# Dilation groups of a head pair in the order 1, 2, 0, and softmax denominators spread over the partitions through DRAM

## The reference, cut to what matters

```python
hn = rmsnorm(x, norm_g)
q, k, v, z_a, hc, gb, gc, z_b, g = split(hn @ w_in)
for gi, (window, dil) in enumerate(((128, 1), (512, 4), (2048, 16))):
    o[gi], lse[gi] = dilated_band_attention(q[gi], k[gi], v[gi], dil, radius=64, slopes[gi])
wts  = softmax(stack(lse), axis=0)          # weight of each group by its denominator
attn = sum_over_gi(wts[gi] * o[gi])         # 8 heads of 64
a = (silu(z_a) * attn) @ w_attn_out
c = (silu(z_b) * (gb * conv3(gc * hc))) @ w_conv_out
merged = sigmoid(g_a) * a + sigmoid(g_c) * c
y = rmsnorm(x + merged @ w_o, final_g)
```

## Time and profile before

| | |
|---|---|
| median of 3 runs | 1641.95 us (1641.55 to 1642.54) |
| profiled execution | 1640.05 us |
| its span on the slowest core (core 3) | 1638.5 us (cores: 1630.6 to 1638.5) |
| PE / DVE / ACT / POOL busy | 1530.7 / 947.4 / 697.9 / 174.1 us |
| mean granted TensorE clock, core 3 | 0.978 |
| PE waits for ACT copies before L737 | 22.4 us |
| reciprocals L777 and L784 | 56.0 + 55.9 us |

### The profile page before, as it was taken

The page is one execution under the profiler, slowest core; times in us unless marked ns, Lnnn a source line. Parts: engine busy times, 40 slices in busy tenths (PEclk is TensorE's granted clock), DMA queues, the critical chain, the costliest instruction groups (busy, mean ns, idle before and its releaser), DMA issues.

```text
span 1638.5 us, 30303 instructions; the slowest of 8 cores (1630.6 to 1638.5 us)
## 1 busy us (share of the span) xinstructions
PE 1530.7 (93%) x12384; PEld 867.6 (53%) x12384; DVE 947.4 (58%) x1438; ACT 697.9 (43%) x1168; POOL 174.1 (11%) x286
## 2 busy tenths in 40 slices
PE   3699999999899999899998999989699999999997
PEld 2354444576556675557665676656344444444443
DVE  2477776335845758558476565675844444444444
ACT  3355444255554455544645446455422222222222
POOL 5111112100000100101001001010300000000001
PEclk9799999999999999999999999999799999999999
DMA  9955455634341432522525205342791322233223
GB/s 192 129 115 111 105 112 93 69 46 66 47 40 17 75 36 57 63 21 50 57 52 69 27 29 72 55 54 29 113 160 62 103 103 78 103 103 103 78 77 142
DMA packets 163371, 127.48 MB, mean 78 GB/s; under 512 B 122912, under 2 KB 144544, under 8 KB 163232
## 3 DMA queue, kind: packets, MB, share of 16 engines
q0 software_dynamic: 118688, 33.56, 22.3%
q1 hardware_dynamic: 44544, 91.98, 19.8%
HBM read 127.03 MB, written 32.05 MB: 97 GB/s over the span
## 4 chain that ended last, share of the span: by engine, by line
PE 78%; DVE 12%; DMA 5%; ACT 3%; issue 2%; POOL 0%; SPq 0%; DVEq 0%; POOLq 0%; ACTq 0%
PE ps L388 45%; PE ps L640 11%; PE ps L938 7%; PE ps L964 6%; PE ps L737 5%; PE ps L704 3%; DVE X L784 3%; DMA wbf<-w_in 2%; ACT X L378 1%; DVE X L717 1%; DVE X L753 1%; DMA gc_s<-X 1%; ACT X L713 1%; DMA X<-xw 1%; DVE X L789 1%
## 5 line engine op out<-in xcount | busy, mean ns | idle before, releaser
L388 PE MATMUL ps<-hnT,wbf 128*128 128x512 bf16 (+2 forms) x3072 | 695.7, 380 | 20.5 <-ACT hnT L378 10.9
L388 PEld LDWEIGHTS ps<-hnT,wbf 128*128 128x128 bf16 x3072 | 291.8, 99 | 353.2 <-issue 28.5
L378 ACT ACTIVATE X<-ps 128x512 bf16<-128x512 f32 (+2 forms) x320 | 214.0, 678 | 248.3 <-PE ps L388 188.6
L717 DVE TENSOR_TENSOR X<-X,et 128x512 bf16<-128x512 bf16 x384 | 158.0, 423 | 239.4 <-ACT X L713 232.5
L713 ACT ACTIVATE X<-ps 128x512 bf16<-128x512 f32 x384 | 207.9, 598 | 167.8 <-PE ps L704 166.0
L388 PE MATMUL ps<-hnT,X 128*128 128x512 bf16 (+1 forms) x1088 | 230.4, 366 | 0.0
L640 PE MATMUL ps<-wbf,hnT 128*128 128x128 bf16 x3744 | 228.3, 222 | 0.0
L640 PEld LDWEIGHTS ps<-wbf,hnT 128*128 128x128 bf16 x3744 | 222.4, 123 | 0.2
L943 DVE SCALAR_TENSOR_TENSOR hnT<-hnT,ps 128x512 f32<-128x512 f32 x128 | 88.0, 687 | 168.5 <-PE ps L938 168.5
L163 POOL DMA_DIRECT2D wbf<-w_in x96 | 84.5, 887 | 817.4 <-PE ps L388 516.4
L399 ACT ACTIVATE X<-X 128x1024 bf16<-128x1024 f32 x80 | 84.3, 1053 | 201.9 <-DVE X L968 178.4
(11 more groups left out here) (44 smaller groups left out, 911.5 us busy)
## 6 DMA issues: line engine op xcount, KB each, us to landing
X<-xw SPq DMA_DIRECT2D x80, 512.0 KB, 5.7
wbf<-w_in POOLq DMA_DIRECT2D x96, 256.0 KB, 8.2
y<-X SPq DMA_DIRECT2D x32, 512.0 KB, 2.9
X<-w_in POOLq DMA_DIRECT2D x16, 256.0 KB, 32.1
ga_s<-X SPq DMA_DIRECT2D x32, 128.0 KB, 3.5
X<-ga_s SPq DMA_DIRECT2D x8, 512.0 KB, 6.9
X<-gc_s SPq DMA_DIRECT2D x8, 512.0 KB, 7.6
gc_s<-X SPq DMA_DIRECT2D x24, 128.0 KB, 5.4
```

The lines of the kernel that those rows point to most:

```text
L378: return op("act", lambda e: e.activation(out=out, in_=in_, func=AF.Copy), reads=reads, writes=writes)
L388: fns.append(lambda e, kt=kt: e.matmul(bv.cols(c0, n), lhsT=wf(kt), rhs=hnT.cols(kt * WT + t0, n), start=(kt == 0), stop=(kt == 7)))
L717: op("dve", lambda e, hh=hh, eoff=eoff: e.tensor_tensor(out=prv.ap(hh * 512, [[256, 2], [1, 256]]), in0=prv.ap(hh * 512, [[256, 2], [1, 25 ...
```

## The change

1. The groups of a head pair run in the order 1, 2, 0 (`GORD`), the weight blocks too. Group 1 is now the one that ACT copies into the accumulator; its items run over `j` first, so that items 0 to 3 write the first 1024 columns of each head and items 4 to 7 the second, and each claims only these two quarters. Group 2 is now added by DVE. No `stage_b` is held back any more.
2. The denominators take another way. Part 0 (at once): two DMAs of 2 KB store one row of each head's denominators to DRAM (`dn_s`), and one DMA reads them back as 8 values on each of 128 partitions. Part 1 (two items later): one reciprocal of 128 x 8 and a DMA to `rc_s`. Part 2 (three items after part 0): two DMAs that read each row of 512 values back onto 64 partitions, then the `za` projection, the tanh and the multiply-add. Part 3 (five items after part 0): the multiplications and the store to `ga_s`. The two ACT copies and the two large reciprocals are gone. All the new DMAs are on SP's queue.
3. Projections are shared out over the items by their columns, not by their number.
4. At the end the parts still pending are taken between the first merge steps (each counts for two items). `wahead(8)` comes after merge step 1, behind the 8 gate blocks of `c_weights_2`; the 8 loads of `w_o` (`c_weights_3`) and the first two `x3_load` come after step 3.

```diff
+    GORD = (1, 2, 0)
+    dn_d = nc.dram_tensor("dn_s", [2 * 1024], F32)
+    rc_d = nc.dram_tensor("rc_s", [2 * 1024], F32)
...
-            for quad in range(4):
-                for j in range(2):
+            qj = [(q_, j_) for j_ in range(2) for q_ in range(4)] if g == 1 else [(q_, j_) for q_ in range(4) for j_ in range(2)]
...
+                        if g == 1:
+                            act_copy(av_.ap(quad + 1024 * j, [[NOWN, 2], [4, 256]]), bv.ap(0, [[256, 2], [1, 256]]),
+                                     [R_bank[ob]], acc_res(2 * j) + acc_res(2 * j + 1))
+                            return
                         if g == 2:
-                            act_copy(av_.ap(4 * quad + 2 * j, [[NOWN, 2], [1, 2], [16, 128]]),
-                                     bv.ap(0, [[256, 2], [128, 2], [1, 128]]), [R_bank[ob]], acc_.r)
-                            return
-                        if g == 1:
-                            av, ares = av_.ap(quad + 1024 * j, [[NOWN, 2], [4, 256]]), acc_.r
+                            av, ares = av_.ap(4 * quad + 2 * j, [[NOWN, 2], [1, 2], [16, 128]]), acc_.r
...
+            def part0():
+                for hh, (c0, p0) in enumerate(((ca, 64), (cb, 0))):
+                    dma("sp", "d_dn%d" % k, bass.AP(dn_d, 1024 * k + 512 * hh, [[512, 1], [1, 512]]),
+                        accV.cols(c0, 512, p0, 1), reads=ares, writes=[R_dn[k]])
+                dma("sp", "d_rl%d" % k, rcpv.ap(8 * k, [[4, 2], [1, 4]]),
+                    bass.AP(dn_d, 1024 * k, [[4, 128], [512, 2], [1, 4]]), reads=[R_dn[k]], writes=[R_rcp[k]])
             def part1():
-                act_copy(rsc.v.cols(0, 512, 0, 64), accV.cols(ca, 512, 64, 64), ares, rsc.r)
-                act_copy(rsc.v.cols(0, 512, 64, 64), accV.cols(cb, 512, 0, 64), ares, rsc.r)
+                op("dve", lambda e: e.reciprocal(out=rc, in_=rc), reads=[R_rcp[k]], writes=[R_rcp[k]])
+                dma("sp", "d_rs%d" % k, bass.AP(rc_d, 1024 * k, [[4, 128], [512, 2], [1, 4]]),
+                    rcpv.ap(8 * k, [[4, 2], [1, 4]]), reads=[R_rcp[k]], writes=[R_rc[k]])
+            def part2():
+                for hh in range(2):
+                    dma("sp", "d_rb%d" % k, rsc.v.cols(0, 512, 64 * hh, 64),
+                        bass.AP(rc_d, 1024 * k + 512 * hh, [[0, 64], [1, 512]]), reads=[R_rc[k]], writes=rsc.r)
                 bk = next_pbank()
                 proj_fm(bk, w_slot(sza), OWN0 + NOWN * h + 512 * cc, 512)
...
-                op("dve", lambda e: e.reciprocal(out=rsc.v.cols(0, 256), in_=rsc.v.cols(0, 256)),
-                   reads=rsc.r, writes=rsc.r)
...
-            def part2():
-                op("dve", lambda e: e.reciprocal(out=rsc.v.cols(256, 256), in_=rsc.v.cols(256, 256)),
-                   reads=rsc.r, writes=rsc.r)
+            def part3():
...
-            return [part1, part2]
+            return [(0, part0), (2, part1), (3, part2), (5, part3)]
...
-                if g == 2:
-                    if i == 2:
-                        assert not fin_pending
-                        do_b(0)
-                        do_b(1)
-                    elif i > 2:
-                        do_b(i - 1)
-                elif i >= 1:
+                if i >= 1:
                     do_b(i - 1)
-                upto = len(nxt) * (i + 1) // nit
-                while pi < upto:
-                    nxt[pi]()
+                while pi < len(nxt) and (i == nit - 1 or spent < total * (i + 1) / nit):
+                    spent += nxt[pi][0]
+                    nxt[pi][1]()
                     pi += 1
+                gi[0] += 1
...
-        for f_ in fin_pending:
-            f_()
-        wahead(8)
-        assert wst["issued"] == len(wblocks)
...
-        x3_load(0)
-        x3_load(1)
...
                 merge_step(c, dt_)
+                if c == 0:
+                    gi[0] += 2
+                    fin_run()
+                    if dt_ == 1:
+                        wahead(8)
+                    if dt_ == 3:
+                        assert not fin
+                        c_weights_3()
+                        x3_load(0)
+                        x3_load(1)
```

More of the change, by code:

```diff
@@ L232, in build_program @@
                          + ["d_la%d" % i for i in range(2)] + ["d_lc%d" % i for i in range(2)]
-                         + ["d_wo%d" % i for i in range(8)])
+                         + ["d_wo%d" % i for i in range(8)]
+                         + ["d_%s%d" % (n_, i) for n_ in ("dn", "rl", "rs", "rb") for i in range(2)])
         for sname in ["s_pe", "s_act", "s_dve", "s_pool"] + dma_sem_names:
@@ L243, in build_program @@
         patt = View(patt_t[:])
+        rcpv = View(rcp_t[:])
         ident = View(cbf_t[:, 128:256])
@@ L274, in build_program @@
         R_patt = Res()
+        R_rcp = [Res(), Res()]
+        R_dn = [Res(), Res()]
+        R_rc = [Res(), Res()]
         R_gad = [[Res() for _ in range(8)] for _ in range(4)]
@@ L346, in build_program @@
             for h in range(NHALF):
-                for g in (2, 1, 0):
+                for g in GORD:
                     for c in (C_Q, C_K, C_V):
@@ L560, in next_pbank @@
             return r[pbank["i"] % len(r)]
-        units = [(hp, h, g) for hp in range(4) for h in range(NHALF) for g in (2, 1, 0)]
+        units = [(hp, h, g) for hp in range(4) for h in range(NHALF) for g in GORD]
         def k_start(g, h):
@@ L591, in start_piece @@
                    reads=[R_patt], writes=vsub(e0, nov))
-            pieces.append(start_piece)
+            pieces.append((0, start_piece))
             def permuted(dst, c, per):
@@ L607, in qpiece @@
                     act_copy(o, bank(bk).ap(0, idims), [R_bank[bk]], qt.r)
-                pieces.append(qpiece)
+                pieces.append((512, qpiece))
             ks = k_start(g, h)
@@ L648, in proj_pieces @@
                 if h:
-                    kl = [kpiece(128 + 512 * c) for c in range(4)]
+                    kl = [(512, kpiece(128 + 512 * c)) for c in range(4)]
                 else:
-                    kl = [kpiece(512 * c) for c in range(4)] + [kpiece(2048, 128)]
+                    kl = [(512, kpiece(512 * c)) for c in range(4)] + [(128, kpiece(2048, 128))]
             else:
-                kl = [kpiece(c) for c in range(nload // 4, nt // 4)]
-            vl = [vpiece(t0, min(4, nt - t0)) for t0 in range(nload, nt, 4)]
+                kl = [(512, kpiece(c)) for c in range(nload // 4, nt // 4)]
+            vl = [(128 * min(4, nt - t0), vpiece(t0, min(4, nt - t0))) for t0 in range(nload, nt, 4)]
             pieces += kl + vl
@@ L661, in proj_pieces @@
             if h == 0:
-                pieces.append(save_piece)
+                pieces.append((0, save_piece))
             return pieces
@@ L683, in tiles @@
                 return 4 * quad + bi, 16 + 4 * quad + bi
-            for quad in range(4):
-                for j in range(2):
+            qj = [(q_, j_) for j_ in range(2) for q_ in range(4)] if g == 1 else [(q_, j_) for q_ in range(4) for j_ in range(2)]
+            for quad, j in qj:
+                if True:
                     st = {}
@@ L838, in build_program, with fin_add, fin_run @@
         load_etab(0)
-        for p in proj_pieces(0, *slots[0]):
+        for _, p in proj_pieces(0, *slots[0]):
             p()
-        fin_pending = []
+        fin = []
+        gi = [0]
+        def fin_add(hp, h, cc):
+            for (lag, fn) in finalize_parts(hp, h, slots[("za", hp, h)], cc):
+                fin.append((gi[0] + lag, fn))
+            fin.sort(key=lambda x: x[0])
+            fin_run()
+        def fin_run():
+            while fin and fin[0][0] <= gi[0]:
+                fin.pop(0)[1]()
         prev_b = [None]
@@ L844, in build_program @@
         for u, (hp, h, g) in enumerate(units):
-            if h == 1 and g == 2 and hp + 1 < 4:
+            if h == 1 and g == GORD[0] and hp + 1 < 4:
                 load_etab(hp + 1)
@@ L859, in build_program @@
             nit = len(items)
-            pi = 0
+            total = sum(c_ for c_, _ in nxt)
+            pi, spent = 0, 0
             def do_b(ib):
@@ L997, in build_program @@
             for dt_ in range(8):
+                if c == 0 and dt_ == 3:
+                    assert wst["issued"] == len(wblocks)
                 merge_step(c, dt_)
+                if c == 0:
+                    gi[0] += 2
+                    fin_run()
+                    if dt_ == 1:
[5 more added lines that the diff above has]
+                        x3_load(1)
                 if c > 0 and dt_ % 2 == 1:
```

15 lines of the change are left out of this document (9 added, 6 removed).

## The result

**The changed kernel is slower.** Its median is 1692.78 us (1690.02 to 1708.98), that of the kernel before, on the same chip, 1642.24. The ratio is 1.0319, with a 95% interval of 1.0291 to 1.0348, so 3.2% slower where 3% faster was forecast. Some executions, of either kernel, run with a whole die at a lower clock; medians here are over all executions of a kernel, ratios leave those out, and where too few others were left the text gives no ratio.

The account below looks back on a forecast made before the run. TensorE was taken as the bound, full except for small holes worth 47 us in the attention. From 1640.05 us, minus 41 there and 8.5 at the last unit, came 1590.6, or 1592 as median; range 1573 to 1617.

Parts of the forecast that it names:

- the way through DRAM: Denominators' six DMAs per quarter on SP's queue: expected to fit the time available, so no cost inside the attention.
- rival 3: Attention: in-order DVE waits for late hops beside other traffic, 30 us slower than now, 1670 us; chance 0.05.
- Edits without a price: Step on reordered pieces, weight blocks and table load, and sharing out by columns: no matmul added or removed, no cost.
- Chain of part 0: Stores and read-back of a quarter's denominators: 5.2 us, 8.8 with slower hops, against two items' time, 7.8 us at shortest.
- SP is idle enough: Claim that SP's queue can take 192 more DMAs, at about 0.32 us per issue.
- the 32 KB rows: Profile rows of small transfers, 1.6 us towards DRAM and 1.8 from it, used as the argument against rival 3.
- The last unit: Last attention unit with merge step 0 and block 87's wait: 34.1 us against 42.6, 8.5 gained (bounds -5 and 15).
- Block 87: Last gate weights, issued behind the eight blocks of c_weights_2: TensorE waits 4.5 us in merge step 3 (bounds 0, 16).
- rival 1: Block 87 lands 16 us late in the merge; the transition gains nothing or loses 3, 1602 us; chance 0.20.
- The size of the gain: Attention holes worth 47 us: 6 left standing, 41 gained (bounds 20 and 47).
- The accumulator's forms: New strided accumulator writes: DVE's addition taken as 1.07 us, ACT's copy bounded by 0.6 and 1.1; price nothing.
- The marks: Listed profile signs: right with head-pair periods of 202 to 205 us; wrong with reciprocal or key waits, periods over 210.

Follow-up runs that it names:

- e9: e7 without its pacing, so weight loads go five and more at once as in the changed kernel: 1640.01 us, ratio 0.9989.
- e7: Changed kernel with DMA pairs in flight together, weight loads one per item, key/value loads earlier, last half finalised as before, last weight slot reassigned: 1613.48 us.
- e10: e7, but the second DMA of each pair again waits for the landing of the first: 1644.15 us, ratio 1.0015.
- e11: e7 with the three ALiBi table loads issued one unit later, out of the chain's way on SP: 1592.03 us, ratio 0.9689.
- e3: Changed kernel with a resource and semaphore for each DMA of a pair, so both are in flight: 1656.18 us in one execution, no ratio.
- e4: Changed kernel with weight loads handed out at most one per item, the end of the attention unchanged: 1671.89 us, ratio 1.0179.
- e2: Changed kernel with the old finalisation (two ACT copies, two large reciprocals) and no way through DRAM: 1627.41 us, ratio 0.9886.
- e6: Changed kernel, but the last half (head pair 3, half 1) finalised the old way: 1667.0 us, ratio 1.0114.

## Why the prediction was wrong, step by step

**The step that failed** is the one on the way through DRAM: "I take nothing for it inside the attention". Its chain of 5.2 us (8.8 at the upper bound) against 7.8 was a sum of hops of 1.6 and 1.8 us. Three things in it were wrong, and the runs give a size to each.

1. *Hops were counted as if nothing else ran.* The rows of 32 KB that I used are medians over the kernel; the chain needs its hop at one place, and there 1.28 MB of keys and values stand ahead on SP's own queue and POOL sends five weight loads: 9.8 and 11.5 us for the read-backs, 11.3 for 4 KB. The price without pacing is 26.5 us (e9 against e7). That POOL issues in bursts stood in the profile of before, as four loads issued at 437.84 behind a wait of 38 us; I had not laid its timeline beside the chain. The hop itself stood there too. SP's loads of keys and values at 440.44 and 440.93, beside that burst, landed so late (KB, us; before, issues in 437 to 465 us):

```profile
X<-v_s SPq DMA_DIRECT2D x1, 192.0 KB, 11.8
X<-k_s SPq DMA_DIRECT2D x1, 128.0 KB, 11.5
```

That is twice the 5.5 us from which rival 3 decides. And the new order puts larger loads at the same place, which "Edits without a price" doesn't mention.

2. *Two hops were counted as one.* "Chain of part 0: 2 x 0.32 + 1.6 + ..." has both stores in flight at once. In the edit both claim `R_dn[k]`, and both read-backs `rsc`, so the second waits until the first has landed: six hops in series where I counted four. This is worth 30.7 us (e10 against e7). A reading of the diff, without any trace, would have shown it.
3. *"SP is idle enough"* counted 0.32 us per issue. In an in-order queue the waits between issues count: SP stood for 147.0 + 93.7 us, with key loads (37.9 us of ACT's waits) and `ga_s` stores behind it, and the three table loads ahead of it (21.5 us, e11 against e7, measured on two chips; the ratios differ by 0.0101, 17 us). The three sizes are taken with the rest mended, so they can't be added up to the loss of the changed kernel; e3 and e4, each mended alone, took back less than the whole.

**Rival 3**, with a chance of 0.05, is what happened: in-order DVE waits for late hops, from about 5.5 us each. It was given 30 us of loss and 50 were measured. Its sum was of the attention alone, 19 against 12 us per head pair or 28 in four, and there 34.1 came; for the end it had nothing, where 20.9 came. Its reason against, "the 32 KB rows", was no reason, since those rows were not read beside the traffic in question.

**The last unit.** Forecast: 8.5 us gained. Measured: 20.9 lost. The sum had DVE waiting for 2 us in quarters 0 and 1; instead TensorE has holes of 12.06, 3.83, 7.30 and, in merge step 3, 7.46 us, all behind DVE waiting for the chain (12.85 us at 1201.42). The loads of `w_ao` and `w_co` (1 MB each, issued at 1181.56 and 1182.53) and from 1205.08 the gate blocks run beside it, with a DMA share of 0.96 in the window above; that they are the cause is argued and not tested, as no run moves them. In e11, with the old way there, the transition takes 53.6 us up to merge step 4 against 58.1 before: 4.5 us gained, within the bounds of -5 and 15.

**Block 87.** In the changed kernel it is issued at 1240, and no wait of TensorE for it is in the profile: the step that needs it starts at 1254.02, held by DVE. With that lateness gone it shows: 8.71 (e2) and 9.35 us (e6), on the slowest cores twice the 4.5 of the sum, between forecast and rival 1.

**What held.** *The size of the gain:* 41 us were forecast for the attention; in e11 the last unit starts at 1105.04, 41.9 us earlier than before. The holes of the earlier trace rows had the cause that was named, and it goes with the reciprocals. That e11 comes to 1592 is still not the forecast come true: it is another kernel. *The small reciprocal:* 0.196 us against 0.2. *DVE:* 845.8 us busy against about 835. *The accumulator's forms:* ACT 1167 ns against bounds of 0.6 and 1.1 (a little above), DVE 1049 against 1.07. That this costs nothing fits, but no run takes the forms out alone. A window of 340 to 390 us, to be held against the earlier trace rows:

```profile
L387 ACT ACTIVATE X<-ps 128x512 f32<-128x512 f32 x6 | 7.0, 1167 | 0.0
...
L764 DVE TENSOR_TENSOR X<-ps,X 128x512 f32<-128x512 f32 x5 | 5.2, 1049 | 0.0
```

*The marks.* The list of what would show it wrong named two of the waits that came (the small reciprocal ended by a DMA, ACT's copies for `k_s`) and periods over 210 us (the score matmuls that are late at 447.16 are so again at 685.92 and 911.18, 239 and 225 us later), and said that small packets far later than the rows would make it most wrong. So the chance of 0.05 and the range up to 1617 didn't fit what I had written down myself. With hops bounded by a median alone, and 8.8 us against 7.8 available at the upper bound, rival 3 should have had several times that chance.

## What to carry to other kernels

Price a DMA that a computation waits for by the landing time beside the traffic of its own moment, and not by a median: lay the timelines of all queues over the stretch, look for bursts of a queue that was held by a buffer and for large loads ahead on the same queue, and count which DMAs of a chain can really be in flight together. On an in-order queue a wait costs everything behind it, so count its waits and not its issues. If a change with a sound idea comes out slower, look at what stands around it: here a handful of edits to resources, issue times and order turned a ratio of 1.032 into 0.969.

## What the runs showed of the hardware

- **Small DMAs under load.** The 4 KB transfers from and to the tile of reciprocals landed in 1.6 us at the least, 2.5 at the median and 11.3 at the most, the last beside the burst of weight loads; all transfers of `rc_s` (the 128 KB read-backs and the 4 KB stores) in 1.6, 3.2 and 13.3, the longest a read-back beside a burst. With the loads spread (e11) the longest of these took 6.5.
- **A queue can get nothing for 5 us.** Between 451 and 456 us of the changed kernel 2363 packets of POOL's queue were moved and none of SP's, though SP had two transfers under way. The rows don't show why.
- **A stride of 16 bytes in float32 pays like a stride of 64.** ACT's copy takes 1167 ns at the stride of 4 elements and 1073 at 16; DVE's addition 1049 in pairs 16 apart and 1070 at every fourth, against 682 contiguous.
- **TensorE's clock** is lower where the holes are: the granted clock over the attention is 0.96 in the changed kernel, 0.98 before and 1.00 in e11; behind the hole that ended at 466.39 us eight value matmuls took 1.03 us where they take 0.61 elsewhere, and the granted clock from 466.39 to 470.00 is 0.50, the lower level.
